# Attention heads: the fifth copy of turned weights on VectorE, the negated maximum in one operation, half of the mixing coefficient a step ahead

## The reference

```python
s = jnp.einsum('bqhnd,bkhnd->bnhqk', q, k) * (1.0 / math.sqrt(HEAD_DIM))
a = jax.nn.softmax(s, axis=-1)
a = a[:, 0] - lam * a[:, 1]
return jnp.einsum('bhqk,bkhv->bqhv', a.astype(v.dtype), v)
```

## Time and profile before

| | |
|---|---|
| median of 3 runs | 3349.25 us (3349.17 to 3351.36) |
| the profiled execution | 3348.51 us |
| its span | 3346.9 us |
| TensorE matmuls busy | 3173.2 us, 95% |
| TensorE weight loads busy | 2961.7 us, 88% |
| VectorE busy | 2200.7 us, 66% |
| ScalarE busy | 1673.0 us, 50% |
| GpSimd busy | 659.0 us, 20% |

### The profile page before, as it was taken

One profiled execution on the slowest core, in us unless ns is written; L12 is line 12 of the kernel. 1 busy time (PEld: TensorE's weight loads), 2 busy tenths in 40 slices (PEclk: granted clock), 3 DMA queues, 4 the chain that ended last, 5 costly groups with the idle time before them and its releaser, 6 DMA issues. The chain is left out here.

```text
span 3346.9 us, 69332 instructions
## 1 busy us (share of the span) xinstructions
PE 3173.2 (95%) x23550; PEld 2961.7 (88%) x23550; DVE 2200.7 (66%) x3720; ACT 1673.0 (50%) x3713; POOL 659.0 (20%) x866
## 2 busy tenths in 40 slices
PE   6989999999999999998988993999999999999998
PEld 4988989988988998997776883999999999999998
DVE  4887777777777777777874446556555555555553
ACT  4656656666666666665652113444443444444442
POOL 2532333233233323331000002011001000000001
PEclk9999999999999999999998996999999999999999
DMA  8663344344434335342326543566666666666653
GB/s 287 240 201 114 113 138 124 115 130 134 125 113 150 113 111 159 113 122 88 106 72 250 196 172 129 167 191 187 196 190 191 192 189 188 189 189 189 184 183 101
DMA packets 373846, 530.68 MB, mean 159 GB/s; under 512 B 29658, under 2 KB 321754, under 8 KB 358490
## 3 DMA queue, kind: packets, MB, share of 16 engines
q1 hardware_dynamic: 363996, 494.52, 45.6%
q0 software_dynamic: 9728, 34.61, 4.6%
HBM read 439.10 MB, written 89.16 MB: 158 GB/s over the span
## 5 line engine op out<-in xcount | busy, mean ns | idle before, releaser
L2544 PE MATMUL ps_gu<-xT,e_w 128*128 128x272 f32 x6144 | 786.2, 290 | 2.1 <-DVE xT L2728 2.1
L2544 PEld LDWEIGHTS ps_gu<-xT,e_w 128*128 128x128 f32 x6144 | 776.8, 188 | 3.2 <-issue 2.3
L2717 DVE TENSOR_TENSOR e_w<-e_raw,e_w 128x2048 fp32r<-128x2048 f32 x189 | 433.0, 2291 | 416.7 <-ACT e_w L2617 402.6
L1059 ACT ACTIVATE e<-ps_s,negm 128x1024 f32<-128x1024 f32 (+2 forms) x416 | 474.3, 1148 | 264.8 <-DVE negm L1423 264.8
L1415 DVE TENSOR_REDUCE mx<-ps_s 128x1 f32<-128x1024 f32 (+3 forms) x428 | 523.7, 1234 | 123.6 <-PE ps_s L732 123.5
L732 PE MATMUL ps_s<-kT,qT 128*128 128x512 f32 (+1 forms) x1920 | 493.5, 389 | 20.1 <-ACT e L1059 10.7
L769 PE MATMUL ps_m<-v,aT 128*128 128x128 f32 x3456 | 458.8, 278 | 0.9 <-ACT aT L1045 0.9
L732 PEld LDWEIGHTS ps_s<-kT,qT 128*128 128x128 f32 x1920 | 340.1, 190 | 127.0 <-ACT e L1059 61.7
L769 PEld LDWEIGHTS ps_m<-v,aT 128*128 128x128 f32 x3456 | 421.4, 192 | 3.5 <-ACT aT L1045 1.1
L2563 PE MATMUL ps_gu<-hid,e_w 128*128 128x272 f32 x3072 | 412.2, 291 | 0.0
L799 PE MATMUL ps_m<-w,hT 128*128 128x384 f32 x2040 | 392.4, 340 | 3.9 <-DVE o L1467 3.9
(11 more groups left out here) (324 smaller groups left out, 3236.3 us busy)
## 6 DMA issues: line engine op xcount, KB each, us to landing
hT<-hT_d SPq DMA_DIRECT2D x85, 1024.0 KB, 5.3
e_raw<-w_gate SPq DMA_DIRECT2D x64, 1024.0 KB, 5.0
e_raw<-w_up SPq DMA_DIRECT2D x64, 1024.0 KB, 5.0
e_raw<-w_down SPq DMA_DIRECT2D x64, 1024.0 KB, 7.4
tab<-tabs_d SPq DMA_DIRECT2D x85, 256.0 KB, 2.7
hT_d<-hT SPq DMA_DIRECT2D x17, 1024.0 KB, 4.0
cat_o<-cat_d SPq DMA_DIRECT2D x17, 1024.0 KB, 5.9
w_lent<-w_ada SPq DMA_DIRECT2D x16, 1024.0 KB, 5.4
```

The costliest lines, as they stand in the source:

```text
L1059: nc.scalar.activation(out, src, ACT.Exp, bias=negm[:, s.par, c:c + 1], scale=HD ** -0.5, accum_out=acc).then_inc(exp_done.sem, 1)
L2544: mm = nc.tensor.matmul(ps_gu[:, 2 * (s % 2) + f, 0:SLOTS], w_view(s, a)[:, k, f * P:f * P + P], xT[:, b, k, :], start=(k == 0 and a + b = ...
L2717: nc.vector.tensor_tensor(w[:, s % RING, 1, :], raw[:, s % RAW, :], w[:, s % RING, 0, :].bitcast(F32), ALU.subtract).then_inc(w_lo, 1)
```

## The change

Three edits, all in `stage_heads`.

- The fifth copy of turned weights (`copy_turned` with n = 4) goes from ScalarE to VectorE (`copy_fifth`) in steps with a sample back of heads 1 to 5. It stands behind `negate(s, 0)` and ahead of `normal_kq`. It has an event of its own, `aT_dve`, for which TensorE waits wherever it waited for the fifth copy.
- `negate` becomes one operation, maximum and product with the negated scale. With three groups (last head) an operation `fold` between the second and third maximum takes the larger of the first two.
- `coefficient` is cut in two. `first_sums`, at the end of the step in which the first pair's exponentials are made, does its row sum l0, the product -lambda l0 and the reciprocals of both, into `rl`, which now has two halves by parity. `coefficient` itself adds the parts of l1, multiplies by the reciprocal of -lambda l0 and takes the reciprocal of that: two linked operations, three in the last head. `evacuate` reads the half of `rl` that belongs to its tile.

```diff
--- before.py
+++ after.py
@@ -237,7 +237,9 @@
         l3 = sb("l3", [P, 2, 2, len(LAST_GROUPS)])
         l3p = sb("l3p", [P, 2, 3])
         l = sb("l", [P, 2])
-        rl = sb("rl", [P, 2])
+        rl = sb("rl", [P, 2, 2])
+        l1 = sb("l1", [P, 1])
+        ratio = sb("ratio", [P, 1])
         coef = sb("coef", [P, 1])
         sq4 = sb("sq4", [P, 4])
         ms4 = sb("ms4", [P, 4])
@@ -318,13 +320,17 @@
             return lambda h, i, front, back, qkv, kq: n if kq else 0
 
         s_ready = event("s_ready", on_groups)
-        mx_part, mx_all, negm_done = event("mx_part", on_groups), event("mx_all", on_front(2, 2)), event("negm_done", on_front(2, 2))
+        mx_part = event("mx_part", lambda h, i, front, back, qkv, kq: on_groups(h, i, front, back, qkv, kq)
+                        + (2 if h == H and front == "sample" else 0))
+        negm_done = event("negm_done", on_front(2, 2))
         exp_done = event("exp_done", on_groups)
 
-        l_sum, l_rec, coef_done = event("l_sum", on_back(1, 1)), event("l_rec", on_back(1, 1)), event("coef_done", on_back(1, 1))
+        l0_steps, coef_done = event("l0_steps", on_front(3, 3)), event("coef_done", on_back(1, 1))
+        l1_steps = event("l1_steps", lambda h, i, front, back, qkv, kq: (2 if h == H and back == "sample" else 1) if back else 0)
         mixed = event("mixed", on_back(5, 1))
         aT_ready, pv_part = event("aT_ready", on_back(5, 1)), event("pv_part", on_back(5, 1))
-        aT_act = event("aT_act", on_back(5, 1))
+        aT_act = event("aT_act", lambda h, i, front, back, qkv, kq: {"sample": 5 if h == H else 4, "prompt": 1, None: 0}[back])
+        aT_dve = event("aT_dve", lambda h, i, front, back, qkv, kq: 1 if back == "sample" and h < H else 0)
         o_done, o_sq_done, oms_done, orr_done, on_done, oT_ready, o_hi, o_lo = (
             event(n, on_back(1, 1)) for n in ("o_done", "o_sq_done", "oms_done", "orr_done", "on_done", "oT_ready", "o_hi", "o_lo"))
         cat_saved = [event(f"cat_saved{q}", on_back(16, 16), q) for q in range(2)]
@@ -675,7 +681,14 @@
             sp.wait_ge(ctx_saved, 32 * H)
 
         def act_copies(s):
-            return {"sample": 5, "prompt": 1, None: 0}[s.back]
+            return {"sample": 5 if s.h == H else 4, "prompt": 1, None: 0}[s.back]
+
+        def dve_copies(s):
+            return 1 if s.back == "sample" and s.h < H else 0
+
+        def maxima_of(s):
+
+            return len(groups_of(s)) + (1 if s.h == H and s.front == "sample" else 0)
 
         def projected(s):
 
...
@@ -757,7 +771,10 @@
 
                 head = s.h - 1 if s.back == "sample" else s.h - 2
                 blocks = TGROUPS[n] if s.back == "sample" else [0]
-                aT_act.wait(pe, s, n + 1)
+                if n == 4 and dve_copies(s):
+                    aT_dve.wait(pe, s, 1)
+                else:
+                    aT_act.wait(pe, s, n + 1)
                 if n == 0:
                     qk_copied.wait(pe, s)
                     v_copied.wait(pe, s)
...
@@ -1385,18 +1405,36 @@
 
         @block.vector
         def _(dve):
+            def first_sums(s):
+
+                exp_done.wait(dve, s, len(groups_of(s)))
+                sums = l3[:, s.par, 0, 0:len(groups_of(s))] if s.front == "sample" else l3p[:, 0, 0:1]
+                nc.vector.tensor_reduce(l[:, 0:1], sums, AX, ALU.add).then_inc(l0_steps.sem, 1)
+                l0_steps.wait(dve, s, 1)
+                nc.vector.tensor_scalar(l[:, 1:2], l[:, 0:1], neglam[:], None, ALU.mult).then_inc(l0_steps.sem, 1)
+                l0_steps.wait(dve, s, 2)
+                o_done.wait(dve, s)
+                nc.vector.reciprocal(rl[:, s.par, :], l[:]).then_inc(l0_steps.sem, 1)
+
             def coefficient(s):
 
-                exp_done.wait(dve, s)
-                sums = l3[:, s.prev_par, :, 0:len(LAST_GROUPS if s.h == H else GROUPS)] if s.back == "sample" else l3p[:, :, 0:1]
-                o_done.wait(dve, s)
-                nc.vector.tensor_reduce(l[:], sums, AX, ALU.add).then_inc(l_sum.sem, 1)
-                l_sum.wait(dve, s, 1)
-                nc.vector.reciprocal(rl[:], l[:]).then_inc(l_rec.sem, 1)
-                l_rec.wait(dve, s, 1)
+                l0_steps.wait(dve, s)
+                over = rl[:, s.prev_par, 1:2]
+                if s.back == "sample":
+                    sums = [l3[:, s.prev_par, 1, n:n + 1] for n in range(3)]
+                    if s.h == H:
+                        exp_done.wait(dve, s, -1)
+                        nc.vector.tensor_scalar(l1[:], sums[0], sums[1], None, ALU.add).then_inc(l1_steps.sem, 1)
+                        l1_steps.wait(dve, s, 1)
+                        sums = [l1[:], sums[2]]
+                    exp_done.wait(dve, s)
+                    nc.vector.tensor_scalar(ratio[:], sums[0], sums[1], over, ALU.add, ALU.mult).then_inc(l1_steps.sem, 1)
+                else:
+                    exp_done.wait(dve, s)
+                    nc.vector.tensor_scalar(ratio[:], l3p[:, 1, 0:1], over, None, ALU.mult).then_inc(l1_steps.sem, 1)
+                l1_steps.wait(dve, s, 2 if s.h == H and s.back == "sample" else 1)
                 mixed.wait(dve, s)
-                nc.vector.scalar_tensor_tensor(coef[:], l[:, 0:1], rl[:, 1:2], neglam[:], ALU.mult,
-                                               ALU.mult).then_inc(coef_done.sem, 1)
+                nc.vector.reciprocal(coef[:], ratio[:]).then_inc(coef_done.sem, 1)
                 coef_done.wait(dve, s, 1)
 
             def mix(s, n):
@@ -1414,14 +1452,29 @@
                 s_ready.wait(dve, s, per * c + n + 1)
                 nc.vector.tensor_reduce(mx[:, c, n:n + 1], ps_s[:, at:at + hi - lo], AX, ALU.max).then_inc(mx_part.sem, 1)
 
+            def fold(s, c):
+
+                mx_part.wait(dve, s, maxima_of(s) * c + 2)
+                nc.vector.tensor_scalar(mxc[:, c:c + 1], mx[:, c, 0:1], mx[:, c, 1:2], None, ALU.max).then_inc(mx_part.sem, 1)
+
             def negate(s, c):
                 per = len(groups_of(s))
-                mx_part.wait(dve, s, per * (c + 1))
-                nc.vector.tensor_reduce(mxc[:, c:c + 1], mx[:, c, 0:per], AX, ALU.max).then_inc(mx_all.sem, 1)
-                mx_all.wait(dve, s, c + 1)
+                mx_part.wait(dve, s, maxima_of(s) * (c + 1))
                 exp_done.wait(dve, s)
-                nc.vector.tensor_scalar(negm[:, s.par, c:c + 1], mxc[:, c:c + 1], -HD ** -0.5, None,
-                                        ALU.mult).then_inc(negm_done.sem, 1)
+                out = negm[:, s.par, c:c + 1]
+                if per == 1:
+                    ins = nc.vector.tensor_scalar(out, mx[:, c, 0:1], -HD ** -0.5, None, ALU.mult)
+                elif per == 2:
+                    ins = nc.vector.tensor_scalar(out, mx[:, c, 0:1], mx[:, c, 1:2], -HD ** -0.5, ALU.max, ALU.mult)
+                else:
+                    ins = nc.vector.tensor_scalar(out, mx[:, c, 2:3], mxc[:, c:c + 1], -HD ** -0.5, ALU.max, ALU.mult)
+                ins.then_inc(negm_done.sem, 1)
+
+            def copy_fifth(s):
+
+                aT_ready.wait(dve, s, 5)
+                pv_part.wait(dve, s, 3)
+                nc.vector.tensor_copy(aT[:, 0, 0:len(TGROUPS[4]) * P], ps_t[:, 0, 0:len(TGROUPS[4]) * P]).then_inc(aT_dve.sem, 1)
 
             def normal_kq(s):
                 r4_done.wait(dve, s, 1)
@@ -1464,7 +1517,7 @@
                 pv_part.wait(dve, s, 5 if s.back == "sample" else 1)
                 on_done.wait(dve, s)
                 o_sq_done.wait(dve, s)
-                nc.vector.tensor_scalar(o[:], ps_m[:, 0:P], rl[:, 0:1], None, ALU.mult).then_inc(o_done.sem, 1)
+                nc.vector.tensor_scalar(o[:], ps_m[:, 0:P], rl[:, s.prev_par, 0:1], None, ALU.mult).then_inc(o_done.sem, 1)
 
             def mean_square(s):
                 o_sq_done.wait(dve, s, 1)
...
@@ -1647,10 +1702,13 @@
                 mix(s, 3)
                 for n in range(len(groups_of(s))):
                     maximum(s, 1, n)
+                    if n == 1:
+                        fold(s, 1)
                 negate(s, 1)
                 if late(p):
                     normal_out(p)
                 mix(s, 4)
+                first_sums(s)
                 if late(p):
                     split_out(p)
                 if s.j is None and s.i == NS:
@@ -1693,10 +1751,14 @@
                 if s.front:
                     for n in range(1, len(groups_of(s))):
                         maximum(s, 0, n)
+                        if n == 1 and s.h == H:
+                            fold(s, 0)
                     negate(s, 0)
                 if s.h == 1 and s.zero:
                     split_rest(1)
                     low_pooled(LATE)
+                if s.back == "sample":
+                    copy_fifth(s)
                 if s.kq:
                     normal_kq(s)
                 if s.back == "sample":
@@ -1708,9 +1770,13 @@
                 if s.front:
                     for n in range(1, len(groups_of(s))):
```

(8 more changed lines are left out.)

## The result

The changed kernel takes 3314.57 us (median of 4 runs, 3313.51 to 3316.08) against 3350.31 us before (4 runs). The ratio is 0.9895 with a 95% interval of 0.9883 to 0.9908: 36 us faster. It was measured twice more beside the experiments, at 0.989 (0.9875 to 0.9906) and 0.9893 (0.9878 to 0.9909). The forecast was 3309 us, range 3302 to 3327. The two profiled executions lie 32.4 us apart (3348.51 and 3316.08 us, the second the longest of its four runs), so what follows from their traces adds up to 32 and not to 36.

What follows compares the result with a forecast made beforehand. PE stands still 0.59 us per step, exponentials queued behind ScalarE's fifth copy. 75 x 0.52 = 39.0, minus 0.8, plus 2.4 gives 40.6 us, taken as 40, from 3349.25: 3309 us; range 3302 to 3327.

Steps and rivals of the forecast that it cites:

- One sign of being right: Ordinary step of the loop: should last 15.0 to 15.15 us after the change, 15.59 before.
- Exponentials 0.52 us sooner: Ordinary steps, ScalarE: without its fifth copy and with shorter negation, both exponentials end at 1075.12 instead of 1075.64.
- The copy on VectorE: Ordinary steps: copy lasts 0.68 us (bounds 0.415 and 0.83), ends at 1073.32; fifth value multiply waits some 0.1 us.
- q and k, POOL: Ordinary steps: POOL's chain starts about 0.45 us later but is covered; parts ready 1078.22, turn 1078.35, slack 0.13 us.
- Rival (a): The turn of q and k becomes the new wait, 0.17 us a step; gain 28 us, time 3322; chance 0.17.
- The coefficient: Ordinary steps: half moved a step ahead; 0.65 us before the first mix becomes about 0.4; costed at nothing.
- i = 16: Front is the prompt, heads 1 to 5: PE waits 0.4 us for parts, coefficient returns 0.25; cost 0.8 us in all.
- i = 0: Both maxima shorten PE's 0.92 us wait for the exponential by 0.4 us; 2.4 us over 6 heads, bounds 0 and 5.5.
- Last head: 16 steps: fifth copy stays, fold replaces reduction, three linked operations remain, sums covered by VectorE's idle 1.39 us: no gain.

## Why the prediction was right, and where its terms were off

The sign, the mechanism and the range were right: the exponentials stood behind ScalarE's own copy; moving it and shortening the negation let the second scores follow at once. The sum was 40.6 us; measured are 36. Two terms were mis-sized, the start of VectorE's copy and what the coefficient is worth once the step is shorter; the others moved less. One sign of being right failed: a step should have lasted 15.0 to 15.15 us, and lasts 15.2. By its steps:

- **Exponentials 0.52 us sooner.** Against the last maximum's end the first exponential starts 0.28 us later now (1052.06 to 1052.34), reckoned 0.25; before it was 0.77 (1072.35 to 1073.12), so the gain is 0.49. The one operation takes 0.214 us where I had 0.15 for it. Small.
- **The copy on VectorE.** Its duration, 0.68 us by the line of the maxima, measures 0.692. The Trainium skill (VectorE: DVE Perf Modes, The TRN2 errata) led to an estimate of 0.66 us: 0.03 us short, but its ranking of the two engines agrees with the trace (0.69 us against 0.58 for the same copy on ScalarE). The term that was mis-sized is the start. I had the copy begin 0.04 us behind the end of the fifth turn (1072.64 for 1072.60), and in the step shown it begins 0.12 us behind (1052.63 for 1051.91 + 0.60 = 1052.51). In the steps that the program has written out, outside of the hardware loop, it begins as I had it, here at i = 2 of head 4:

```profile
1021.61 0.60 PE L767 MATMUL ps_t<-ident,e 128*128 128x128 f32 x4
...
1022.25 0.69 DVE L1477 COPY aT<-ps_t 128x512 f32<-128x512 f32 x1 [0.68 <-PE ps_t L767]
```

  Of the copies that waited for the turn, all 57 in the loop begin late and all 18 outside of it do not. TensorE's wait for the copy, 58 places, is in the loop alone. So the copy ends 0.1 us later than reckoned behind its turn (0.81 us for 0.72), and the second scores with it: they are all loaded 4.50 us behind the start of the fifth turn (1051.91 to 1056.41) where it was 4.92 (1072.00 to 1076.92). That is 0.42 us gained a step, reckoned 0.52, and 7.5 us over 75 steps. The step as a whole is 15.59 - 15.21 = 0.38 us shorter in the one compared, 0.43 in the median of all ordinary steps.
- **q and k, POOL.** The chain was covered in ordinary steps, as said. The parts are there at 1057.39 + 0.74 = 1058.13, their turn loads at 1058.37. Rival (a) did not come.
- **The coefficient.** Its two operations take 0.27 and 0.17 us, not twice 0.2 with the hand-over, and 1061.19 to 1061.79 is 0.6 us, not 0.4. "No PE wait hangs on it in an ordinary step" was true of the kernel before, where the wait at the first turn cost nothing, and false of the changed one. I checked the slack at the old pace. Once the step is 0.4 us shorter, three linked operations leave the turn 0.13 us late in every second step, and the third part saves that. It was costed at nothing and is worth 3.7 us.
- **i = 16.** The wait of 0.4 us at the turn of q and k came as worked out. The coefficient's 0.25 us did not: the step got 0.48 us longer (13.07 to 13.55), not 0.15. With ScalarE making the copy there it is still 0.1 us longer than before (five steps, 0.5 us). The rows, first before, then after, are the starts of the first scores at i = 15, 16, 0 and 1:

```profile
976.53 1.51 PEld L732 LDWEIGHTS ps_s<-kT,qT 128*128 128x128 f32 x7
...
992.30 0.52 PEld L732 LDWEIGHTS ps_s<-kTp,qTp 128*128 128x128 f32 x4 [0.16 <-issue]
...
1005.37 0.82 PEld L732 LDWEIGHTS ps_s<-kT,qT 128*128 128x128 f32 x4
...
1018.64 1.51 PEld L732 LDWEIGHTS ps_s<-kT,qT 128*128 128x128 f32 x7
```

```profile
958.24 1.51 PEld L745 LDWEIGHTS ps_s<-kT,qT 128*128 128x128 f32 x7
...
973.42 0.52 PEld L745 LDWEIGHTS ps_s<-kTp,qTp 128*128 128x128 f32 x4
...
984.45 0.42 PEld L844 LDWEIGHTS ps_t<-ident,parts 128*128 128x128 f32 x4 [0.42 <-issue]
...
986.97 0.82 PEld L745 LDWEIGHTS ps_s<-kT,qT 128*128 128x128 f32 x4
...
999.96 1.51 PEld L745 LDWEIGHTS ps_s<-kT,qT 128*128 128x128 f32 x7
```

- **i = 0.** 0.28 us gained (13.27 to 12.99), reckoned 0.4. Heads 2 to 5 show the same; head 1 loses 0.27 us and head 6 nothing clear, so it is 0.8 us in all and not 2.4. The negated maximum alone gives the same 0.28.
- **Last head.** Reckoned at nothing. The fold, which stands ahead of the third maximum, and the one operation behind it:

```profile
1601.92 0.21 DVE L1458 TENSOR_SCALAR mxc<-mx 128x1 f32<-128x1 f32 x1
...
1602.51 0.21 DVE L1470 TENSOR_SCALAR negm<-mx,mxc 128x1 f32<-128x1 f32 x1
```

From the first maximum (1599.53) to the end of the negation (1602.72) are 3.19 us; before it was 3.06 (1629.76 to 1632.82). Both operations with two columns take 0.21 us where the pair they replace takes 0.16 and 0.15. From the first to the last product of `modulation_half` the last head took 200.2 us before, 203.1 in the changed kernel's first trace, 202.6 and 200.8 in the two others. Over all kernels, the ten traces with the fold have 200.6 to 203.5 us (mean 201.8), the four without it 198.5 to 202.2 (mean 200.1). The new sums alone show 198.5, so they are covered, as reckoned. A loss of 1 to 2 us by the fold is likely and not settled, since the two groups overlap; it was not tried alone.

The terms in one line, counted in the trace from first scores to first scores: the 75 ordinary steps give 34.4 us (0.46 on average, with the third part's share in it), i = 16 takes 2.4 (5 x 0.49), i = 0 gives 0.8, and all else together changes it by 0.3 us: 32.5 us of the span, 3346.9 to 3314.4. The two other traces of the changed kernel have 36.5 and 37.0, of which 1.6 us are one step of head 1 and some 2 us lie behind heads 1 to 5; what makes these differ is not known.

## What to carry to other kernels

When one engine both serves TensorE and starts the next long chain, look at what stands in its queue between the input being ready and the long operation starting: here 0.4 us of a copy, paid 75 times, was worth two thirds of the gain, while shortening the other engine's chain alone was worth almost nothing. Let a consumer start on the first half of a copy; that gave another 11 us. A line in a list of waits is not yet a cost: 7.5 us stood there before and cost nothing, and the same wait, 0.14 us longer in the faster kernel without the third part, cost some 4 us. So check each slack again at the new pace, in both kinds of step of a loop that holds two.

## What the runs showed of the hardware that was not expected

- The same instruction starts 0.12 us behind the matmul that it waits for in the hardware loop (1052.51 to 1052.63) and 0.04 us behind it in steps written out (1022.21 to 1022.25); ScalarE's copy started 0.03 us behind its turn (1072.60 to 1072.63 in the earlier trace rows). Matmul ends are modelled, so it is the difference of the two that counts. What makes the start later in the loop is not shown by any row. It comes to 57 x 0.09 = 5 us, an estimate from these rows, and no run tried to get it back.
- A `tensor_scalar` on one column takes 0.154 us when its only operand from memory is that column (L1423 before), 0.214 us with a second (L1468) and 0.273 us with a third (L1431); group rows of the changed kernel, heads 1 to 5 and the start of the last:

```profile
L1477 DVE COPY aT<-ps_t 128x512 f32<-128x512 f32 x80 | 55.3, 692 | 33.7 <-PE ps_t L767 32.2
...
L1468 DVE TENSOR_SCALAR negm<-mx 128x1 f32<-128x1 f32 x157 | 33.6, 214 | 5.6
```

- Parts do not add up. Alone they give 23, 3 and 2 us, together 36. With the copy out of the way the second gives 7 (same comparison) and the third 3.7.
